# Value/gate product and both output projections by one level of Strassen's scheme, in a fused retention + sliding-window kernel

## What is computed

```python
# x: (1, 2048, 1024); one retention layer, then one sliding-window layer
def retention_layer(x, w_in, w_out, pos):
    q, k, v, g = split(x @ w_in, [1024, 2048, 4096])      # w_in 1024 x 6144
    q, k = rope(q), rope(k) * 256 ** -0.5                 # 4 heads of 256
    # v, g: 4 heads of 512; chunkwise retention: inner part + carried state
    r = normalise(inner(q, k, v) + cross(q, state))       # per head, state 256 x 512
    return (silu(g) * r) @ w_out                          # w_out 2048 x 1024
def swa_layer(x, w_in, w_out, sinks, k_band, v_band, bias, key_valid):
    q, gate = split(x @ w_in, 2)                          # w_in 1024 x 2048
    o = softmax_with_sink(q @ k_band + bias) @ v_band     # 16 heads, 4 kv heads, band 128
    return (o * silu(gate)) @ w_out                       # w_out 1024 x 1024
x = post_norm(x, retention_layer(x, ...))
k_sh, v_sh = split(x @ swa_w_kv, 2)                       # 1024 x 512
x = post_norm(x, swa_layer(x, ...))
```

## Time and profile before

| | |
|---|---|
| median of 3 runs | 2561.5 us (2561.47 to 2563.3) |
| profiled execution: own time / span | 2563.65 us / 2561.9 us |
| mean granted TensorE clock | 0.987 |
| busy: TensorE, VectorE, ScalarE, GpSimd | 96%, 62%, 34%, 21% |
| moved by DMA | 242.5 MB, mean 95 GB/s |

### The profile page before, as it was taken

How to read it: one execution, slowest core, us unless ns; L and a number is a source line. 1 busy time by engine, 2 the same in 40 slices (tenths; PEclk the granted TensorE clock), 3 DMA queues, 4 the chain that set the end, 5 groups by cost and what they waited for, 6 DMA issues and landing times.

```text
span 2561.9 us, 30304 instructions
## 1 busy us (share of the span) xinstructions
PE 2471.6 (96%) x11986; PEld 2016.7 (79%) x11986; DVE 1600.9 (62%) x2381; ACT 859.9 (34%) x1114; POOL 549.8 (21%) x424
## 2 busy tenths in 40 slices
PE   7999999999999999999999999999999999999996
PEld 6888887778788888787778888878777888887775
DVE  6576644486865764548676576454867656645577
ACT  3333332244333332235423333223433333222352
POOL 3132311121431231102133122120213322212022
PEclk9999999999999999999999999999999999999998
DMA  5222223413322222331332222323133222232413
GB/s 170 76 66 82 91 91 116 120 61 116 115 66 75 74 91 99 115 108 57 116 115 69 80 75 91 110 97 115 59 111 120 82 75 67 90 135 71 122 68 132
DMA packets 137757, 242.52 MB, mean 95 GB/s; under 512 B 9424, under 2 KB 44768, under 8 KB 137616
## 3 DMA queue, kind: packets, MB, share of 16 engines
q1 hardware_dynamic: 137104, 239.25, 28.3%
q0 software_dynamic: 512, 1.34, 0.3%
HBM read 227.18 MB, written 9.18 MB: 92 GB/s over the span
## 4 chain that ended last, share of the span: by engine, by line
PE 63%; DVE 15%; issue 14%; DMA 4%; ACT 2%; POOL 1%; SPq 0%; DVEq 0%; ACTq 0%
PE acc L469 16%; PE acc L470 16%; PE acc L471 16%; DMA stage<-ret_w_in 3%; DVE w_lo L908 3%; PE bank L471 3%; PE bank L470 3%; PE bank L469 3%; PE bank L665 2%; DVE qrT L345 2%; ACT w_hi L732 1%; PE bank L674 1%; PE bank L531 1%; PE bank L684 1%; DVE sg L340 1%
## 5 line engine op out<-in xcount | busy, mean ns | idle before, releaser
L908 DVE TENSOR_TENSOR w_lo<-stage,w_hi 128x1024 fp32r<-128x1024 f32 x372 | 472.8, 1273 | 419.7 <-ACT w_hi L732 414.5
L469 PE MATMUL acc<-w_hi,actT_hi 128*128 128x512 f32 (+1 forms) x1408 | 548.2, 389 | 38.3 <-DVE v_lo L1103 14.6
L732 ACT ACTIVATE w_hi<-stage 128x1024 fp32r<-128x1024 f32 x372 | 391.6, 1055 | 486.6 <-PE acc L471 375.9
L471 PE MATMUL acc<-w_hi,actT_lo 128*128 128x512 f32 (+1 forms) x1408 | 539.4, 383 | 0.0
L470 PE MATMUL acc<-w_lo,actT_hi 128*128 128x512 f32 (+1 forms) x1408 | 538.9, 383 | 0.0
L469 PE MATMUL acc<-actT_hi,w_hi 128*128 128x512 f32 x1088 | 443.0, 407 | 16.5 <-DVE actT_lo L934 9.8
L470 PE MATMUL acc<-actT_lo,w_hi 128*128 128x512 f32 x1088 | 429.8, 395 | 0.0
L471 PE MATMUL acc<-actT_hi,w_lo 128*128 128x512 f32 x1088 | 428.4, 394 | 0.0
L469 PEld LDWEIGHTS acc<-w_hi,actT_hi 128*128 128x128 f32 x1408 | 268.5, 191 | 95.1 <-DVE w_lo L908 36.1
L1227 POOL TENSOR_TENSOR rstd<-ve,half 128x1 f32<-128x1 f32 x96 | 63.0, 656 | 1259.1 <-DVE ve L949 764.2
L471 PEld LDWEIGHTS acc<-w_hi,actT_lo 128*128 128x128 f32 x1408 | 268.5, 191 | 51.0
(11 more groups left out here) (127 smaller groups left out, 3243.4 us busy)
## 6 DMA issues: line engine op xcount, KB each, us to landing
stage<-ret_w_in SPq DMA_DIRECT2D x130, 512.0 KB, 3.7
stage<-ret_w_in SPq DMA_DIRECT2D x136, 256.0 KB, 2.9
stage<-ret_w_out SPq DMA_DIRECT2D x64, 512.0 KB, 3.3
stage<-swa_w_in SPq DMA_DIRECT2D x64, 512.0 KB, 3.6
stage<-swa_w_out SPq DMA_DIRECT2D x32, 512.0 KB, 3.3
xbuf<-x_turned SPq DMA_DIRECT2D x20, 512.0 KB, 5.1
z<-x_pad SPq DMA_DIRECT2D x16, 512.0 KB, 4.1
stage<-swa_w_kv SPq DMA_DIRECT2D x16, 512.0 KB, 3.2
```

The costliest lines, as they stand in the source:

```text
L469: nc.tensor.matmul(dst, lhs[0], rhs[0], start=start, stop=False)
L471: return nc.tensor.matmul(dst, lhs[1], rhs[0], start=False, stop=stop)
L732: nc.scalar.activation(w_hi[:, q % RING], stage[:, q % STAGES], ACT.Copy).then_inc(w_hi_made.sem, 1)
L908: nc.vector.tensor_tensor(w_lo[:, q % RING], stage[:, q % STAGES], w_hi[:, q % RING].bitcast(F32), ALU.subtract).then_inc(w_split.sem, 1)
```

## The change

Each 2 x 2 block product C = A B (A: two token halves of 256 by two halves of k, B: two halves of k by two halves of columns) is made with seven products P1 to P7 instead of eight. It is used three times: `vg` (per head, the column halves are v and g, k halves of 512), `ro` (k halves of 1024) and `so` (k halves of 512). The keys of `kv` are also made in two token halves, so 256 columns wide.

- **TensorE**: a weight pair of a Strassen product now feeds 12 matmuls of 512 columns (`strassen_pair`: 2 token tiles x 2 k-slices x 3). A block has 134 pairs: per head 4 q/k + 14 vg, 28 ro, 4 kv, 16 q and gate, 14 so. 512-column matmuls into `acc` in the program: 8640 before, 7776 now; 256-column ones: 384 before, 768 now.
- **Weight sums**: P6, P5, P4 and P7 need sums of weight blocks. In block s = 0 they are made once, 28 sets of 1 MB, kept in HBM (`t_prep`), and loaded like weights afterwards: `load_t` (two DMAs issued by GpSimd), `make_t` (four additions of 128x512; sets 0 to 3 on VectorE, 24 on GpSimd) and a store.
- **Activation sums**: GpSimd makes sums of x, of r and of o (`x_sums`, `r_sum`), 4, 8 and 4 additions of 128x1024 a block. ScalarE and VectorE split them (`split_x_sum` 4, `split_ro` 14, `split_so` 8 a block). The separate splits of turned r (L922, 16 a block) are gone.
- **Partial results**: v and g are sums of two accumulations each (`v_raw`, `sg`: a ScalarE copy, then a VectorE addition); for the outputs they are added onto `z` (`onto_z`, `more_z`).
- **Order**: retention moves to every third vg pair (v places 7, 10, 13, and the next head's second pair). Layer norm goes two tiles at a time (`ln_pair`): tiles 0 and 1 before the last product P4 has ended, tiles 2 and 3 of the second norm at the first pair of the next block.
- **Memory**: `w_lo` is written over `stage` (five slots), loads go four pairs ahead; rope is four instructions (tables with the decay factors in, two of them 128x1024) where it was seven; two heads' state is in SBUF at a time, stored to and loaded from HBM.

```diff
-PAIRS = [(b, kind, c, k, K) for b, (kind, c, K) in enumerate(BLOCKS) for k in range(0, K, 2)]
+VG_ORDER = ("P1", "P2", "P6", "P5", "P7", "P4", "P3")
+OUT_ORDER = ("P1", "P2", "P6", "P5", "P7", "P3", "P4")
+PAIRS = []
+for _h in range(RH):
+    PAIRS += [("qk", _h, None, i) for i in range(4)]
+    PAIRS += [("vg", _h, q, i) for q in VG_ORDER for i in range(2)]
+PAIRS += [("ro", 0, q, i) for q in OUT_ORDER for i in range(4)]
+PAIRS += [("kv", 0, None, i) for i in range(4)]
+for _kind in ("q", "gate"):
+    for _c in range(2):
+        PAIRS += [(_kind, _c, None, i) for i in range(4)]
+PAIRS += [("so", 0, q, i) for q in OUT_ORDER for i in range(2)]
+HS, LS = 4, 5
+AHEAD, LOAD_AHEAD = 3, 4
...
+                for j in range(2):
+                    m, js = bank_of(q, j), slice(j * P, (j + 1) * P)
+                    if i == 0:
+                        need(pe, acc_free[m], prior(s, p, m))
+                    for u in range(2):
+                        k = 2 * i + u
+                        mm = mm3(acc[m][:], (lhs(0, k, js), lhs(1, k, js)), weights(g, u), k == 0 and q in OPENS,
+                                 i == last and u == 1, True)
+                    mm.then_inc(products, 1)
...
+                    if h < RH and j in (VG + 7, VG + 10, VG + 13):
+                        t = (j - VG - 7) // 3
+                        retain(H, t)
+                        score(H, t + 1)
+                            if 1 <= h < RH and (j, u) == (1, 0):
+                                retain(H - 1, 3)
...
+                link(nc.vector.tensor_tensor(q_tmp[:], qrT[:], both(1), ALU.mult))
+                link(nc.vector.tensor_tensor(qrT[:], qrT[:], both(0), ALU.mult))
+                nc.vector.tensor_tensor(qrT[:, 0, :], qrT[:, 0, :], q_tmp[:, 1, :], sub)
+                nc.vector.tensor_tensor(qrT[:, 1, :], qrT[:, 1, :], q_tmp[:, 0, :], add).then_inc(q_roped, 1)
...
+            def make_t(n):
+                b = t_buf[T_BUF[n]]
+                pool.wait_ge(t_loaded[T_BUF[n]], 32 * T_NTH[n])
+                link(tt(b[:, 1, 1, :], b[:, 1, 1, :], b[:, 0, 1, :], sub))
+                link(tt(b[:, 0, 1, :], b[:, 0, 1, :], b[:, 0, 0, :], sub))
+                link(tt(b[:, 0, 0, :], b[:, 1, 1, :], b[:, 0, 0, :], add))
+                link(tt(b[:, 1, 0, :], b[:, 1, 0, :], b[:, 0, 0, :], sub))
+                pool.dma_start(t_prep[n], b[:].rearrange("p u j n -> p (u j) n")).then_inc(t_stored[T_BUF[n]], 16)
+            def x_sums(s):
...
+                tt(s3_tmp[:], x_part(s, 0, 0), x_part(s, 0, 1), sub).then_inc(x_summed, 1)
+                pool.wait_ge(x_summed, 4 * s + 1)
+                tt(s2_tmp[:], x_part(s, 1, 1), s3_tmp[:], sub).then_inc(x_summed, 1)
...
+            def output_sums(s, kind, p):
...
+                if i == 6 * n - 1:
+                    for t in range(2):
+                        more_z(s, first + 6 * n - 1, "P3", "P6", t, 1)
+                if i == 7 * n - 1:
+                    for t in (2, 3):
+                        onto_z(s, first + 7 * n - 1, "P4", t, 0)
...
+                    if p < 2 and s > 0:
+                        split_x(s, 2 + p)
+                    if p == 0 and s > 0:
+                        ln_pair(s - 1, 1, 2)
...
+                        if v == 3:
+                            for i in range(2):
+                                dve.wait_ge(products, full(s, p, i))
+                                dve.wait_ge(acc_free[i], emptied(s, first_pair("vg", h, "P1"), i))
+                                nc.vector.tensor_tensor(v_raw[:, i, :], v_raw[:, i, :], acc[2 + i][:], add)\
+                                    .then_inc(acc_free[2 + i], 1)
```

2044 lines of the change are left out of this document (1199 added, 845 removed).

## The result

The changed kernel takes 2690.8 us (median of 4 runs, 2685.2 to 2699.0) against 2562.0 for the kernel before, measured together with it: ratio 1.0505, interval 1.0474 to 1.0535. It is **129 us slower**; 44 us faster was forecast, and the time is above the forecast's range.

What follows compares the result with a forecast made beforehand. TensorE, busy 96%, was taken to bound the kernel. Terms -150.6 + 50 + 16 + 10 + 21 - 16 + 30 - 4 gave -43.6 us, so a median of 2518 us, range 2425 to 2585.

Steps and rivals of the forecast that it cites:

- Matmuls, -150.6: TensorE, whole program: 672 fewer 512-column matmuls save 152.5 us, narrower key matmuls add 1.9, together -150.6 us.
- Each head, rope, +3.1 each: Each head: TensorE stops 2.3 us at rope and 1.9 before retention, 4.2 against 1.1 now; +50 us over 16 heads.
- ro, +4: Pairs 5 to 12 of ro: VectorE's work and waits for GpSimd's r sums outlast the lead, +4 us four times, +16.
- so, +2.5: Start of so: P2 needs SiLU, gating and splits, about 7.0 us where P1 covers 5.4; +2.5 us four times, +10.
- ro to kv, -4: From ro to kv: earlier norms and narrower key matmuls take back 4 us of idle and lost clock, four times, -16.
- Seam, +7: Block to block: x's low parts come late, 10 us of stops plus 2 against 5 now; +7 at three seams, +21.
- First block, +30: First block: making weight sums adds 6 us at the start and 8 a head, +30 us (+5 to +80).
- Rival C: First block bound by transfers or GpSimd: no loss at 389 GB/s, 55 us more at 246, giving 2573; chance 0.11.
- Rival B: Stops in every head lower TensorE's clock: 16 x 3.4 = 54 us on top, 2572 us; chance 0.12.
- VectorE over 90% in vg: Condition under which the whole forecast falls: VectorE, not TensorE, turns out busy above 90% in vg.
- less 16 and 4: Two savings in the sum: -16 us from ro to kv, -4 at the program's end, with two tiles left, not four.

## Why the prediction was wrong

The step that failed most is the first block's term: it counted 17 us of room on VectorE in a head as a cover for the weight sums and took 30 us where they cost 110. The smaller steps are the seam's, which named the wrong wait, and the clock, which was not in the sum.

- **Matmuls, -150.6.** Right: -149 by the distances between starts.
- **Each head, rope, +3.1 each.** Right in place, size and releaser for heads in mid-block (4.3 us of stops for 4.2, interval 82.8 for 82.5); that is one interval of three. Mis-sized for the last head (6.4 for 2.3; GpSimd's first two sums of r, 5.55 us, follow k's rope directly, and in the run with them later the stop is 2.1) and for the first (4.6, with the splits of the sums of x ahead of rope).
- **ro, +4; so, +2.5.** Stops of 3.5, 0.6, 0.6 and 1.7 us make 6.4, and 2.5, 1.8 and 0.8 make 5.1. Both too small.
- **ro to kv, -4.** Wrong in sign: 3.6 us before the turns of x1 (GpSimd's share of the norm), 0.75 and 2.2 at the keys, 6.5 us of stops where 5.7 stood before.
- **Seam, +7.** Right in size (10 + 1.7 + 1.9 = 13.6 us of stops, 12 forecast), wrong in who is late. The step was "the next block's second pair of x waits for its low part"; it is the accumulator bank of P4, behind a norm that VectorE starts first. That an order could put such a stop right was tried three times: the 22 to 26 us of idle time stayed, while eight low parts less took 8 us off. The forecast also counted VectorE's splits at 1.22 us each there, and beside GpSimd they take 2.3 to 3.4, which no term had; over the program `w_lo` grew by 295 us of VectorE's time instead of 209, its mean from 1273 to 1443 ns.
- **The four terms of a block together.** From last head to next block the forecast makes 24 x 4 x 0.227 = 21.8 less for matmuls, +0.5 for keys, +3.1, +4, +2.5, +7 and -4: -8.7. Measured +11.4 in blocks 1 and 2. The 20 us between are, roughly (the parts make 21.5), 4.1 and 2.3 for the two ropes, 2.4 for ro, 2.6 for so, 1.6 for the seam, 1.5 for kv by its stops, and some 7 for the clock (matmuls at 0.43 us cost 9 to 11 us of such a stretch, 3 before). No one of these terms explains the miss; all are off to the same side.
- **First block, +30.** The largest miss: what it was to cover is worth 110 us. "63 of 80 us leaves 17 a head" took room on an engine for a cover. The room is no use when the work that is needed next stands behind a store that has to land or behind a doubled `att_lo`; and at the start VectorE's own sixteen additions stood ahead of a copy (15.2 us). The term also had GpSimd's additions at 4.2 us a set (6.1 measured) and had the stores' landing nowhere: the diff shows it (`wait_stored` in `load_t`), and what stands behind it in GpSimd's queue is a root that VectorE waits for. Rival C came nearest: its sign, a first block over 50 us longer than the second, holds (325 us for 253 in three head intervals), and its 55 us are two thirds of the 80 that were missing. Its mechanism is borne out for GpSimd and the wait for its stores; a bound by transfers alone is not shown, since the DMA engines are busy 60 to 72% of these intervals (92% at the start, where VectorE's additions hold TensorE up first).
- **The clock, not in the sum.** Rival B had it at 0.12. Stops cost clock, though not where B put them: the head's window still shows 1.00. The long stops do it: 0.77 around the seam's stop of 10 us, 0.91 in block 0. 38 spells at 1.2 GHz, 261 us, against 9 and 70. Over the runs slow time grows with idle time: 159 us at 191 of idle (no sums), 261 at 272, 489 at 472 (ring of four). Against the kernel before, 212 us more of stops came with 63 us more of slow matmuls: a microsecond of stop costs about 1.3 in this kernel. The Trainium skill (TensorE: Matmul & The Clock Gate, section "What's actually happening") has the slow clock as the state that activity lifts, and the rows agree.
- **Why it fell as a whole.** VectorE over 90% in vg, which was to bring it down, did not occur: it is 71% there. It is 94% around the seam, part of it held up by GpSimd. The gain of 149 us was sized right; of the 282 us against it the forecast had 107 (+50, +16, +10, +21, +30, less 16 and 4). Of the 175 missing, 80 are block 0's weight sums, some 45 the clock outside the start and heads of block 0 (55 us after, 9 before), and the 50 that are left many small stops.

What stays open: what the first head interval's 14 us over the run without sums are made of (no part taken out alone brought it under 97.5 us); whether the seam would empty with GpSimd's norm and sums of x out of VectorE's way, since 15 of VectorE's busy us there are spent beside them, a rival to the amount of work that no run tests; and whether a seam with less work for VectorE by another division of the norm (more of it on ScalarE) would keep its gain; this was not tried.

## What to carry to other kernels

When TensorE's work per weight shrinks, find the stretch where the engine that makes the weights is fullest, not its mean over a phase, and sum its work there against TensorE's. Here three new orders of a full stretch brought nothing and less work did. Look first whether the engine is full of its own work or held up by another: compare the durations with the same instructions elsewhere. Room on an engine hides work only if nothing needed sooner is queued behind it; for every wait that is added to an in-order queue (above all one for a store to land) name the next instruction of that queue and who stands still for it. Moving the wait to another queue moves the price with it (GpSimd's heads shrank by 12 to 14 us, SyncE's first one grew by 17). And price stops with the clock they cost, here about 0.3 us for each us.

## What had not been expected of the hardware

- One slot of a ring of loads is worth 295 us in one direction and nothing in the other: 2985.7, 2690.8 and 2693.4 us with four, five and six.
- Instructions of VectorE that read only SBUF are held up beside GpSimd, small ones by more than their own length: 128x128 `att_lo` 720 ns for 280, the one-input cast `att_hi` 614 for 356, 128x1024 `w_lo` 1705 for 1289; the state's sum, which reads PSUM, is unchanged at 684. At the seam a `w_lo` takes up to 3.41 us, and all of it counts as busy.
- GpSimd's own additions of 128x512 took 1.3 us or, in the same set, over 2.1 (1.29 beside 2.14, 1.25 beside 2.22; means 1.3 to 1.6), where a 128x512 product took 1.04 before.
- In a stop of 10 us the clock falls, and the matmuls behind it start 0.43 us apart: the window of 15 us around it shows 0.77.
